# The skip term of a state-space mixer, moved from a separate product into the diagonal of the chunk weights

## The reference

```python
decay  = exp(where(tri, a_cum[l] - a_cum[s], -inf))       # 1 on the diagonal
cb     = einsum('bclgn,bcsgn->bclsg', C, B)
y_diag = einsum('bclsgk,bcsgkp->bclgkp', cb * decay, x * dt)
y_off  = einsum('bclgn,bcgkpn,bclgk->bclgkp', C, h_prev, exp(a_cum))
y      = y_diag + y_off                                   # forwards and backwards, added
y      = y + x * d_skip[:, None]                          # the skip term: one number for each head
y      = rms(y * silu(z)) * norm_g
```

## Time and profile before

| | |
|---|---|
| median of 3 runs | 2570.71 us (2567.81 to 2574.24) |
| the profiled execution | 2571.34 us |
| its span, first to last instruction | 2569.3 us |
| mean granted clock of PE | 0.939 of full speed |
| busy, share of the span | PE 88%, PEld 70%, DVE 58%, ACT 44%, POOL 24% |
| the state-space groups | about 300 to 1410 us of the span |
| L1229 on DVE, L1102 on POOL | 80 times each |
| L1210 on DVE | 320 times |

### The profile page before, as it was taken

How to read it: one execution, slowest core, us unless ns; L and a number is a source line. 1 busy time by engine, 2 the same in 40 slices (tenths; PEclk the granted TensorE clock), 3 DMA queues, 4 the chain that set the end, 5 groups by cost and what they waited for, 6 DMA issues and landing times. The chain is left out here.

```text
span 2569.3 us, 36389 instructions
## 1 busy us (share of the span) xinstructions
PE 2258.7 (88%) x12794; PEld 1811.3 (70%) x12794; DVE 1490.7 (58%) x3267; ACT 1122.4 (44%) x2838; POOL 612.8 (24%) x594
## 2 busy tenths in 40 slices
PE   5769999989999998989886799759999999999686
PEld 1318777778787877878674678647788787877465
DVE  1554595968769595977848422162545554555442
ACT  1414564736465463746544311153444444444321
POOL 0012443535344352635333000021111111110000
PEclk8889999999999999999987899969999999999798
DMA  7561001010100101010000643131112121211153
GB/s 248 201 179 48 33 18 50 17 50 25 42 26 17 50 26 41 26 42 26 29 9 25 218 131 99 50 116 42 49 59 67 50 55 53 66 50 42 44 165 94
DMA packets 117260, 172.05 MB, mean 67 GB/s; under 512 B 27577, under 2 KB 78009, under 8 KB 116825
## 3 DMA queue, kind: packets, MB, share of 16 engines
q1 hardware_dynamic: 117080, 169.73, 21.3%
HBM read 141.53 MB, written 30.13 MB: 67 GB/s over the span
## 5 line engine op out<-in xcount | busy, mean ns | idle before, releaser
L599 PE MATMUL sg_pP<-h_h_hi,sg_whi 128*128 128x512 f32 (+1 forms) x1152 | 417.1, 362 | 14.2 <-POOL sg_wlo L1042 14.2
L600 PE MATMUL sg_pP<-h_h_lo,sg_whi 128*128 128x512 f32 (+1 forms) x1152 | 411.4, 357 | 0.0
L601 PE MATMUL sg_pP<-h_h_hi,sg_wlo 128*128 128x512 f32 (+1 forms) x1152 | 411.0, 357 | 0.0
L599 PE MATMUL at_pP<-h_h_hi,at_whi 128*128 128x512 f32 (+1 forms) x640 | 254.0, 397 | 13.2 <-POOL at_wlo L1837 13.2
L599 PEld LDWEIGHTS sg_pP<-h_h_hi,sg_whi 128*128 128x128 f32 x1152 | 221.9, 193 | 44.7 <-POOL sg_wlo L1042 14.3
L600 PEld LDWEIGHTS sg_pP<-h_h_lo,sg_whi 128*128 128x128 f32 x1152 | 221.6, 192 | 30.2
L601 PEld LDWEIGHTS sg_pP<-h_h_hi,sg_wlo 128*128 128x128 f32 x1152 | 221.1, 192 | 30.6
L601 PE MATMUL at_pP<-h_h_hi,at_wlo 128*128 128x512 f32 (+1 forms) x640 | 238.6, 373 | 0.0
L600 PE MATMUL at_pP<-h_h_lo,at_whi 128*128 128x512 f32 (+1 forms) x640 | 237.2, 371 | 0.0
L1837 POOL TENSOR_TENSOR at_wlo<-at_wr,at_whi 128x1024 fp32r<-128x1024 f32 x32 | 76.3, 2385 | 564.9 <-ACT at_whi L1747 564.9
L1385 PE MATMUL op_pa<-op_whi,op_yhi 128*128 128x512 f32 x448 | 144.6, 405 | 51.5 <-DVE op_ylo L1442 51.5
(11 more groups left out here) (226 smaller groups left out, 4908.1 us busy)
## 6 DMA issues: line engine op xcount, KB each, us to landing
sg_wr<-in_w_ssd SPq DMA_DIRECT2D x48, 512.0 KB, 3.4
at_wr<-in_w_na SPq DMA_DIRECT2D x32, 512.0 KB, 3.5
at_bias<-bt SPq DMA_DIRECT2D x256, 64.0 KB, 2.3
op_yr<-y SPq DMA_DIRECT2D x10, 1024.0 KB, 7.5
md_mod_w<-in_ada_w SPq DMA_DIRECT2D x4, 2048.0 KB, 13.4
nt_mod_w<-in_ada_w SPq DMA_DIRECT2D x4, 2048.0 KB, 10.2
ts_mod_w<-in_ada_w SPq DMA_DIRECT2D x4, 2048.0 KB, 14.8
y<-sg_Z SPq DMA_DIRECT2D x16, 512.0 KB, 3.0
```

Source lines behind the costliest of these rows:

```text
L599: pe.matmul(out, w_hi[:, k, :], h_hi[:, k, t0:t0 + n], start=(k == 0), stop=False)
L600: pe.matmul(out, w_hi[:, k, :], h_lo[:, k, t0:t0 + n], start=False, stop=False)
L601: x = pe.matmul(out, w_lo[:, k, :], h_hi[:, k, t0:t0 + n], start=False, stop=(k == KT - 1))
```

## The change

The four heads' weights W get `ident * d_skip[head]` added by four new DVE operations at the head of `masked`, ahead of the four that are there. Since the decay on the diagonal is exp(0) = 1, the later product E * W leaves this term as it is, and PE's matmul of x with E carries the skip term into pY. A new semaphore skp orders the second four behind the first four, which they overwrite in place. POOL's product xD (L1102), its tile, its wait for yoS and DVE's addition L1229 with the wait L1228 go. L1227 now signals yoS itself and is followed by no wait.

```diff
-        xD = m.sb("xD", [P, 2, UN])
...
-                n = g * NCH + c
-                if n >= 2:
-                    pool.wait_ge(yoS, n - 1)
-                pool.tensor_tensor(heads(xD[:, n % 2, :].rearrange("p (h c) -> p h c", c=HD)), xth(g, c),
-                                   heads(dsk[:, g * HPG:(g + 1) * HPG].unsqueeze(2)
-                                         .to_broadcast([P, HPG, HD])), ALU.mult).then_inc(xDs, 1)
...
                 dve.wait_ge(wfw, n + 1)
                 dve.wait_ge(tri, 2 * n + 2)
+
+                for k in range(HPG):
+                    x = dve.scalar_tensor_tensor(W[:, k, :], ident[:, :], dsk[:, g * HPG + k:g * HPG + k + 1],
+                                                 W[:, k, :], ALU.mult, ALU.add)
+                x.then_inc(skp, 1)
+                dve.wait_ge(skp, n + 1)
                 for k in range(HPG):
                     x = dve.scalar_tensor_tensor(W[:, k, :], cbm[:, :], tab[:, g % 2, DT, c, HPG + k:HPG + k + 1],
                                                  W[:, k, :], ALU.mult, ALU.add)
...
-                chain(dve.tensor_tensor(yo[:, 0:HPG, :], yo[:, 0:HPG, :], yo[:, HPG:H8, :], ALU.add))
-                dve.wait_ge(xDs, n + 1)
-                dve.tensor_tensor(yo[:, 0:HPG, :], yo[:, 0:HPG, :], h3(xD[:, n % 2, :]), ALU.add).then_inc(yoS, 1)
+                dve.tensor_tensor(yo[:, 0:HPG, :], yo[:, 0:HPG, :], yo[:, HPG:H8, :], ALU.add).then_inc(yoS, 1)
```

More of the change, by code:

```diff
@@ L693, in ssd_groups @@
         (small, con, whs, wls, pj, pev, t0s, cv, tnh, sil, tA, evA, xdA, stA, scA, auh, aul, arg, ex, mm_,
-         wch, yoff, yoS, yd, xdF, xDs, stF, scF, ysum, fin1, sqs, ssm, vr, rs, dg, bcs, fin, vch, tri, wfw) = map(m.sem, (
+         wch, yoff, yoS, yd, xdF, skp, stF, scF, ysum, fin1, sqs, ssm, vr, rs, dg, bcs, fin, vch, tri, wfw) = map(m.sem, (
              "small", "con", "whs", "wls", "pj", "pev", "t0s", "cv", "tnh", "sil", "tA", "evA", "xdA", "stA",
-             "scA", "auh", "aul", "arg", "ex", "mm", "wch", "yoff", "yoS", "yd", "xdF", "xDs", "stF", "scF",
+             "scA", "auh", "aul", "arg", "ex", "mm", "wch", "yoff", "yoS", "yd", "xdF", "skp", "stF", "scF",
              "ysum", "fin1", "sqs", "ssm", "vr", "rs", "dg", "bcs", "fin", "vch", "tri", "wfw"))
```

## The result

The changed kernel takes 2593.99 us (median of 4 runs, 2590.23 to 2598.5) beside 2569.26 us of the kernel before in the same rounds: a ratio of 1.0097, 95% interval 1.0067 to 1.0127. A repetition gave 2594.3 beside 2570.13 us, 1.0092 (1.0078 to 1.0106). It is slower, by 24 to 25 us. Predicted were 2603 us, some 32 more than before, with a range of 2586 to 2622: the direction and the range hold, and the size was put too high, 32 us for 24.7 by the medians. The profiled execution took 2597.5 us, 26.2 more than that of before, and it is this difference that is taken apart here.

What follows compares the result with a forecast made beforehand. DVE's stream was taken as the bound in forward slots 0 to 7. Seven groups gave 26.7 us, slot 8 without idle time in two groups 1.9, group 7 3.4: 32 us over 2571.34, so 2603, range 2586 to 2622.

Steps and rivals of the forecast that it cites:

- The price of a set: Four added DVE operations of 128x128 and their wait, ten times a group, 80 in all: 1.24 us each time.
- rival of serial operations: Each of the four new DVE operations waits until the one before has ended: 19 us more, 2622, chance 0.03.
- What L1229 gives back: DVE time saved per slot: 0.46 us without POOL, 0.75 in slots 1, 2, 4, 5, 0.34 in 3, 6, 7.
- inheritance: With L1229 gone, L1239 must wait for POOL's second product instead; 0.75 us saved in slots 1, 2, 4 and 5.
- rival without inheritance: L1239 does not take over L1229's wait for POOL, so a slot costs 1.24 less 1.07: 2579 to 2588, chance 0.10.
- In slot 1 the term: Forward slot 1: 1.24 us added, less 0.75 for L1229 and 0.36 for L1210 freed from POOL, giving +0.13.
- What POOL gives back: Without POOL's 80 products DVE saves 0.41 us at L1200 in slots 3 and 6, and 0.36 at L1210 in slot 1.
- no relief: POOL's dropped work frees nothing on DVE beyond 0.46 us a slot: 80 x 0.78, up to 2633, chance 0.05.
- cover by PE's projection: Slot 8: about 0.96 us of DVE's idle time, in five of seven groups, would be filled by the added work.
- The clock: PE idles more, so one more 1.2 GHz stretch comes in each group: 14 us, 2616, chance 0.15.
- the tenth set: The four added operations in the last backward slot: between nothing and +0.84 us, the middle, +0.4, taken.
- Group 7: The last group, with shorter slots: 12.4 us added, less L1229's and POOL's savings and 2.6 of DVE waits, +3.4.

Runs made afterwards that it cites:

- e1_add_only: The kernel before plus the four new DVE operations and their wait, with the old POOL product and DVE addition kept: 2658.45 us, ratio 1.034.
- e2_drop_both: The kernel before without POOL's product L1102 and DVE's addition L1229, nothing put in their place: 2513.93 us, ratio 0.9782.
- e3_drop_dve: The kernel before without DVE's addition L1229 alone, POOL's product still computed but read by nobody: 2533.52 us, ratio 0.9846.
- e7_after_pool_kept: The changed kernel with POOL's skip product kept and read by nobody: 2622.98 us against 2594.3 for the changed kernel, ratio 1.0207 to before.

## Why the prediction was right, and where a size was off

**What bounds the kernel.** Right. DVE's stream decides in slots 0 to 7: e1_add_only and e2_drop_both nearly add up, and every set put in comes out (1.10 us of 1.17). PE's waits for yo fell by 11.2 us and those for diag and Z grew by 13.9 and 11.5.

**The price of a set.** Predicted 1.24 us, measured 1.17 to 1.18. The 1.13 of the four was right. The 1.24 took with it the 0.10 us in front of L1218, which stands behind the semaphore of L1210 before and after alike and was no part of the addition; the wait for skp itself costs 0.04. Over 80 sets that is 80 x 0.07 = 5.6 us too much, the largest error of the sum. The rival of serial operations is refuted by the same row: the four take 1.14 us, as the four of L1210 did. L1236 starts at 797.76 in slot 4, 0.08 us before L1226 ends. The Trainium skill ("VectorE: DVE Perf Modes", section "The DRAIN you can't avoid"), by which the next operation doesn't start until the pipe is empty, would have it otherwise for this pair. The same section adds that an operation that isn't held back starts earlier, and with that the row agrees; the prediction quoted the first half alone.

**What L1229 gives back.** 0.46 us without POOL in the way: right where it can be read by itself, slot 8 of the two groups without a low stretch, +0.71 for 1.18 less 0.46, and L854 of slot 9, which comes 0.46 earlier. The 37.2 us of e3_drop_dve are 0.46 for each of 80 as well, but that is a coincidence, a mean of slots between -2.6 and +1.4. 0.75 us with inheritance in slots 2, 4 and 5: right, L1236 takes 1.26 us, even over the 1.15 that was forecast. The rival without inheritance is refuted by that row. Its bound had a slip: 14 us less the freed L1200 and L1210, 8.3, is 6 and not 8. In slot 1 the term was wrong. There the prediction carried slot 4's rows over. Slot 1's own timeline was at hand (the earlier trace rows is one line of it) and shows L1239 at 1.26 us where slot 4 has 0.83; the relief was 1.33 + 0.36 = 1.69 us and not 1.11, some 4 us over seven groups.

**What POOL gives back.** L1200's 0.41 us in slots 3 and 6: right. Slot 3's stall beside the 128x1024 product was costed at nothing more and grew by 0.35 us, but L1218 fell there from 0.92 to 0.69, which was not forecast either. The two nearly cancel, so that +0.54 in both slots stands beside +0.49. The rival "no relief", up to 2633, is refuted by e7_after_pool_kept: the relief there is 28.7 us.

**Slots 7, 0 and 8.** Slot 7, +0.85 for +0.90, and slot 8 of the two groups without cover, +0.71 for +0.78, are right but for the price. Slot 0, +0.65 for +0.78, is right by luck. There L1239 took 1.26 us before beside POOL and L1236 takes 0.41 now, the second operation of the new set takes 1.12 instead, and the 128x1024 product holds up another operation than before; none of this was in the sum. Slot 8 of the other five was put at -0.18 and came out at -0.65. The step that failed there was to take the 0.96 us of idle DVE for cover by PE's projection. It was a backlog of PE from the 1.2 GHz stretch in slot 7, 1.36 us long (8.42 less 7.06), and in the changed kernel it doesn't reach slot 8.

**The clock.** As a rival it asked for one more low stretch in each group, 14 us. The stretches came: from slot 0 of group 0 to slot 0 of group 7 the clock records have 54.6 us at the low level before and 78.5 after, seven more pieces of 3.4 us. The cost didn't. Before, it was 1.36 us in slot 8 of five groups and 1.7 in the backward slots of three, 11.9 us. After, ten pieces stand in forward slots that DVE bounds, where no slot with one is more than 0.1 us longer than its like in another group, and one stands behind slot 8 in each of six groups, 1.7 us, with 1.1 more in the seventh, 11.3 us. So the rival had the count right and the price wrong, and the forecast, which left the clock out, was helped by two changes of 6 to 7 us that cancel. These figures are worked out from slot lengths; no run held the clock fixed. The mean clock of the span fell all the same, 0.939 to 0.932: where DVE binds, PE can be slower without the end moving.

**The backward slots.** Predicted were -0.46 for slot 9, -0.20 for the start of it and +0.4 for the tenth set: -0.26 for a group. The -0.46 is right by the rows of L855 and L854. For the rest, +0.2, nothing can be seen: from L855 or L854 to slot 0, groups with a low stretch in the backward slots take 60.7 to 61.0 us before and 60.8 to 60.9 after. Measured were +3.0 us in seven groups all the same, since the low stretches there went from three to six and grew in the seventh, 3 x 1.7 + 1.1 = 6.2 us, less 7 x 0.46. Group 7 was put at +3.4, and came out at +2.3.

**The sum.** Over slots 0 to 8 of the first seven groups the prediction has 30.5 us (5 x 4.08 + 2 x 5.04) and the trace 20.8: 9.7 too much, of which 4.4 are the set's price (0.07 x 9 x 7), 4.1 slot 1, and 2 slot 8; the other slots take nearly 1 back. Behind slot 8 it has -1.8 and the trace +3.0, 4.8 too little, and group 7 is 1.1 too high. That makes 32.0 against 26.1. So the errors cancel in part, by luck: without the one behind slot 8 the change would have been put 10.8 us too high, and not 6.

**What changed in the profile.** Of the signs listed ahead, these came: L1229 and L1102 gone, four new ones in 1.14 us, L1239 at over 1.15, L1200 of slot 3 back, slot 4 at 9.22 us (9.3 forecast), no wait of L1248 in slot 8, PE's wait gone over to diag. These did not, or in part: PE's wait for yo fell by a third but did not vanish, a group's forward part grew by 2.6 to 3.0 us in the five groups and not by 4, and the backward part is not the same.

## What to carry to other kernels

Price an added operation by the start-to-start distance in a slot where nothing else runs, leave out the gap behind a semaphore that stands there anyway, and price a removed one slot by slot: what it waited for is inherited by the next operation. Before idle time is counted as cover, look at the clock in the stretch ahead of it: it may be a backlog that the change removes. Before a term is moved to another place, count its instructions: one 128x512 operation took 0.8 us where four of 128x128 had 1.9 us in all with the stalls, and the sign of the whole change hung on that. Where one engine is the bound and another idles, as PE did for 8% here, the same term may be nearly free there.

## What the runs showed of the hardware

POOL and DVE take turns. L1226 and L1236 follow one another on DVE without a pause in slot 4, POOL's product starts at 797.51 us while L1226 runs, and L1236 behind it takes 1.26 us where it takes 0.42 alone. The Trainium skill ("SBUF — State Buffer", section "🔬 SBUF: two separate sides") has DVE and GpSimd share a port pair under an exclusive lock held for a whole instruction. The trace agrees for operations with two SBUF sources, and L1238, one of whose sources is in PSUM, stays at 0.42 beside POOL's 0.79 us product.

What POOL's work costs therefore isn't a number of its own. The same 80 products of xD, about 0.7 us each, cost 6.7 us in the kernel before, about 19 without L1229 and 28.7 in the changed kernel, because they then meet other operations of DVE and, in the second case, because slot 8 is longer in three groups behind a low stretch.

The stretches at the lower clock move with the length of a slot: from the end of slot 7 before to slot 6 and to the turn to the backward slots after, in most of the seven groups. Ahead of the one at the turn of group 3 PE was busy 6.17 of 7.76 us in slot 8 and then waited 1.56 us for Z. What a stretch costs depends on who binds in it and on whether PE catches up before it is needed: 1.36 us in slot 7 before, paid in slot 8; 1.6 to 1.7 us in the backward slots, where PE is full; next to nothing in slot 6 of the changed kernel's group 3 (clock 0.50, DVE busy 1.97 of 2.00 us), which takes 12.20 us beside 12.11 in group 0, which has none there.
